# Decoder trunk on eight cores: squares of two chunks added in float32 before the ones product, in three of five norms

## The reference, cut to what matters

```python
def rmsnorm(x, g):
    xf = x.astype(jnp.float32)
    y = xf * lax.rsqrt(jnp.mean(xf * xf, axis=-1, keepdims=True) + EPS)
    return (y * g.astype(jnp.float32)).astype(x.dtype)
...
        h = rmsnorm(x, pre_mix_g[i])
        proj = h @ w_in[i] + b_in[i]
...
        x = x + rmsnorm(merged @ w_o[i], post_mix_g[i])
        h = rmsnorm(x, pre_ffn_g[i])
        f = jnp.square(jax.nn.relu(h @ w_ff1[i])) @ w_ff2[i]
        x = x + rmsnorm(f, post_ffn_g[i])
        gate = jax.nn.sigmoid(x @ w_ple_gate[i])
        e = p[i] @ w_ple_proj[i]
        x = x + rmsnorm(gate * e, post_ple_g[i])
```

## Time and profile before

| what | value |
|---|---|
| median of 3 runs | 2176.4 us (2175.73 to 2386.89) |
| the profiled execution's own time | 2177.32 us |
| its span on the slowest core (core 2) | 2175.4 us (2170.3 to 2175.4 over the cores) |
| TensorE busy | 2075.9 us (95% of the span) |
| VectorE busy | 1016.7 us (47%) |
| ScalarE busy | 848.1 us (39%) |

### The profile page before, as it was taken

One profiled execution on the slowest core, in us unless ns is written; L12 is line 12 of the kernel. 1 busy time (PEld: TensorE's weight loads), 2 busy tenths in 40 slices (PEclk: granted clock), 3 DMA queues, 4 the chain that ended last, 5 costly groups with the idle time before them and its releaser, 6 DMA issues.

```text
span 2175.4 us, 30026 instructions; the slowest of 8 cores (2170.3 to 2175.4 us)
## 1 busy us (share of the span) xinstructions
PE 2075.9 (95%) x10640; PEld 1043.8 (48%) x10818; DVE 1016.7 (47%) x1607; ACT 848.1 (39%) x1344; POOL 82.1 (4%) x156
## 2 busy tenths in 40 slices
PE   2999999999899999999989999999999999999996
PEld 1546666676544444444434444444444344444442
DVE  2438555302673856430374565541066385553027
ACT  2345154312645307321374522631166451543125
POOL 0000000000000000000000000000000000000000
PEclk8999999999999999999999999999999999999998
DMA  8234454434444363455576453554343344445342
GB/s 188 41 50 77 75 82 69 72 65 68 89 77 64 53 97 59 74 92 78 106 171 159 67 87 60 85 90 78 59 82 64 63 84 78 78 69 90 56 78 78
DMA packets 36325, 176.82 MB, mean 81 GB/s; under 512 B 3282, under 2 KB 6482, under 8 KB 18770
## 3 DMA queue, kind: packets, MB, share of 16 engines
q0 software_dynamic: 22912, 148.92, 42.6%
q1 hardware_dynamic: 13268, 25.98, 4.0%
HBM read 315.40 MB, written 8.39 MB: 149 GB/s over the span
## 4 chain that ended last, share of the span: by engine, by line
PE 92%; DMA 3%; ACT 2%; issue 2%; DVE 1%; SPq 0%; DVEq 0%; ACTq 0%; POOLq 0%
PE PS L676 80%; PE PS L794 5%; PE PS L593 3%; DMA XB<-xT 2%; PE PS L798 1%; PE PS L898 1%; PE PS L1108 1%; DMA WB<-wst 1%; PE PS L881 1%; ACT L1098 0%; PE PS L565 0%; ACT TMP L1098 0%; DVE U0A L906 0%; DVE XB L994 0%; ACT U1B L635 0%
## 5 line engine op out<-in xcount | busy, mean ns | idle before, releaser
L676 PE MATMUL PS<-U0A,WB 128*128 128x512 bf16 (+2 forms) x2907 | 525.5, 338 | 51.8 <-ACT U3A L833 22.6
L676 PE MATMUL PS<-U0B,WB 128*128 128x512 bf16 x2252 | 503.1, 379 | 3.1 <-ACT U56B L737 0.4
L676 PEld LDWEIGHTS PS<-U0A,WB 128*128 128x128 bf16 x2944 | 289.6, 99 | 271.4 <-issue 60.7
L676 PEld LDWEIGHTS PS<-U0B,WB 128*128 128x128 bf16 x2304 | 224.0, 98 | 264.2 <-issue 1.4
L1024 ACT ACTIVATE TMP<-PS 128x512 f32<-128x512 f32 (+1 forms) x256 | 151.3, 598 | 250.2 <-PE PS L676 245.4
L952 ACT ACTIVATE U1A<-PS 128x512 bf16<-128x512 f32 (+1 forms) x64 | 37.3, 603 | 391.6 <-PE PS L676 391.6
L487 POOL DMA_DIRECT2D WB<-wst x144 | 76.3, 530 | 2028.4 <-PE PS L676 1580.2
L676 PE MATMUL PS<-U2A,WB 128*128 128x512 bf16 (+1 forms) x631 | 120.5, 337 | 0.5
L676 PE MATMUL PS<-U3A,WB 128*128 128x512 bf16 (+1 forms) x637 | 118.0, 338 | 0.2
L676 PE MATMUL PS<-U2B,WB 128*128 128x512 bf16 x498 | 116.8, 379 | 0.9
L676 PE MATMUL PS<-U3B,WB 128*128 128x512 bf16 x504 | 117.1, 379 | 0.4
(11 more groups left out here) (184 smaller groups left out, 2242.1 us busy)
## 6 DMA issues: line engine op xcount, KB each, us to landing
WB<-wst POOLq DMA_DIRECT2D x136, 1024.0 KB, 10.8
XB<-xT SPq DMA_DIRECT2D x2, 2048.0 KB, 37.6
WB<-wst POOLq DMA_DIRECT2D x8, 512.0 KB, 6.3
outT<-XA SPq DMA_DIRECT2D x16, 256.0 KB, 2.9
outT<-XB SPq DMA_DIRECT2D x16, 256.0 KB, 6.9
XA<-xT SPq DMA_DIRECT2D x4, 528.0 KB, 9.4
U2A<-wsT SPq DMA_DIRECT2D x4, 512.0 KB, 6.2
BF<-bsbc SPq DMA_DIRECT2D x4, 512.0 KB, 7.0
```

The source lines that it names most:

```text
L676: return lambda e: e.matmul(PS[:, bk, 0:w], WB[:, b, k * kstride + fi * 128: k * kstride + (fi + 1) * 128], rhs(k, c0, c0 + w), start=(k = ...
```

## The change

Both sets of squares that are touched are now written by a method `square`. It writes the square of chunk dc in float32 into one of two scratch slots (dc even: the first, dc odd: the second), and after each odd chunk VectorE adds the two slots and writes the sum in bfloat16 as chunk dc // 2 of U1. The two slots are the upper half of U1 (chunks 4 to 7), seen as float32. `tail_ones` multiplies 4 chunks instead of 8 in post_mix, pre_ffn and post_ffn. Premix and post_ple keep their 8 products, and so does the sum over the halo. The eviction's other reader (L956 or L960) is unchanged.

```diff
-        def tail_ones(sq, rsq, cbl):
+        def tail_ones(sq, rsq, cbl, nc=8):
             bks = banks(len(cbl))
-            for dc in range(8):
+            for dc in range(nc):
                 fns = [lambda e, bk=bk, dc=dc, c0=c0, w=w: e.matmul(
-                    PS[:, bk, 0:w], ONEB[:], sq(dc, c0, c0 + w), start=(dc == 0), stop=(dc == 7))
+                    PS[:, bk, 0:w], ONEB[:], sq(dc, c0, c0 + w), start=(dc == 0), stop=(dc == nc - 1))
...
+            def square(self, dc, a, b, src, reads, psum, cbl, rp=()):
+                S = self.S
+                two = S.U[1].bitcast(F32).rearrange("p (c t) -> p c t", c=4)
+                t = [two[:, 2 + i, a - S.off[1]: b - S.off[1]] for i in range(2)]
+                rt = [S.rU[1][4 + 2 * i: 6 + 2 * i] for i in range(2)]
+                i = dc % 2
+                P.op("act", act_ns(b - a, psum), lambda e: e.activation(out=sv(t[i], cbl), in_=src, func=AF.Square),
+                     reads=reads, writes=rt[i] + list(rp))
+                if i:
+                    P.op("dve", dve_ns(b - a, False), lambda e: e.tensor_tensor(
+                        out=self.sq(dc // 2, a, b), in0=t[0], in1=t[1], op=ALU.add),
+                        reads=rt[0] + rt[1], writes=self.rsq(dc // 2))
...
@@ evac_O
-                P.op("act", act_ns(self.n, True), lambda e: e.activation(
-                    out=sv(self.sq(oc, a, b), self.cbs), in_=ps(bks, self.cbs), func=AF.Square),
-                    reads=rp, writes=self.rsq(oc) + rp)
+                self.square(oc, a, b, ps(bks, self.cbs), rp, True, self.cbs, rp)
...
@@ norm, post_mix, post_ple
-                bks = tail_ones(self.sq, self.rsq, self.cbs)
+                bks = tail_ones(self.sq, self.rsq, self.cbs, nc)
...
-                self.norm()
+                self.norm(4)
...
-                self.norm()
+                self.norm(8)
...
@@ ffn_eps
-                    P.op("act", act_ns(self.n, False), lambda e, dc=dc: e.activation(
-                        out=self.sq(dc, a, b), in_=S.x(dc, a, b), func=AF.Square), reads=[S.rX[dc]], writes=self.rsq(dc))
+                    self.square(dc, a, b, S.x(dc, a, b), [S.rX[dc]], False, blocks(a, a + 1))
...
@@ ffn_eps2, post_ffn
-                bks = tail_ones(self.sq, self.rsq, self.cbs)
+                bks = tail_ones(self.sq, self.rsq, self.cbs, 4)
```

More of the change, by code:

```diff
@@ L969, in o_half, with norm @@
                 w_done(S)
-            def norm(self):
+            def norm(self, nc):
                 S = self.S
                 a, b = self.r
-                bks = tail_ones(self.sq, self.rsq, self.cbs)
+                bks = tail_ones(self.sq, self.rsq, self.cbs, nc)
                 rsqrt_of(S.rb(a, b), S.rRB, bks, self.cbs)
```

## The result

| | before | after |
|---|---|---|
| profiled execution | 2177.32 us | 2157.07 us |
| median of the runs | 2176.4 us (first three) | 2157.9 us (2157.07 to 2158.86, 4 runs) |
| ratio to before, 95% interval | | 0.9917 (0.9893 to 0.9941) |
| TensorE, VectorE, ScalarE busy | 2075.9, 1016.7, 848.1 us | 2067.8, 1077.9, 848.2 us |

The kernel is 0.8% faster, which is less than the 2% that are held to tell two kernels apart by themselves, but the interval leaves out 1.

What follows compares the result with a forecast made beforehand. Behind the start-up, TensorE's list of matmuls was taken to bound the kernel. 2177.32 - 20.9 (matmuls) + 0.7 (ends of sums) + 0.6 (slots and plan) = 2157.7 us, median 0.9 us lower: 2157 us, range 2151 to 2173.

Steps and rivals of the forecast that it cites:

- Matmuls removed: In three norms of each of 8 passes, 84 wide and 24 narrow matmuls go from TensorE's list: 20.9 us.
- What bounds the kernel: Behind the start-up, TensorE's list of matmuls sets the length, with 2.6% idle; time taken off it shows in full.
- swallowed: Rival: something keeping its own time, such as a weight transfer, ends each stretch, so nothing gets shorter: 2176 us, chance 0.05.
- Squares and adds: ScalarE's squares into float32 cost 9 ns more at most; 96 VectorE adds of 0.69 us, 66 us, VectorE to about 1083.
- The wait at the end of a sum: Last add before the fourth product needs 1.05 us; cover 1.51, or 0.69 behind narrow matmuls: 0.7 us of waits together.
- The two scratch slots: Behind the outer half, third and fourth squares come up to 1.05 us later, hidden; 0.6 us allowed for planner errors.
- my second rival: Scratch pair blocks ScalarE in each round's B.o_half, adds queueing behind two residual operations: 41 us lost, 2198 us, chance 0.07.
- VectorE where it is full: B.o_half and 851.2 to 870.0 us of each round fill up; h has 3.3 and 4.8 us to absorb the backlog.
- the first rival: Adds come late behind 1.2 us residual operations in VectorE's full stretches, two sums a round: 10 us, 2167 us, chance 0.22.
- Sum: Whole kernel: 2177.32 - 20.9 + 0.7 + 0.6 = 2157.7 us, median 2157 us, 0.9% faster; this forecast's chance 0.66.
- What can be told from no change: All cases lie within 2% (2132.9 to 2219.9 us), about what a measurement can tell from no change: chance 0.97.
- TensorE busy about 21 us less: Sign expected in the profile after: TensorE's busy time falls about 21 us, with only tenths of new waits for VectorE.

Runs made afterwards that it cites:

- products alone: Changed kernel without its adds, squares written as before the change, those of chunks 4 to 7 left out of the four-product sums: 2154.99 us, ratio 0.9908 to before.
- Adds alone: Changed kernel with its adds kept but eight products per sum, each added chunk multiplied twice by a matrix of halves: 2177.6 us, ratio 1.0012 to before.

## Why the prediction was right or wrong

The time came out, and two things in the prediction did not: the cost of the new waits, 0.7 us at the ends of sums and 0.6 us for the slots and the plan, where 2.4 us were measured, because the cover was counted from the last square and not along the chain of four pairs through two slots; and the view that a gain of 0.9% is about what a measurement can't tell from none.

- *Matmuls removed, 20.9 us:* right. The counts are as forecast (112 in stream B; 108 fewer in all), and products alone gave 20.0 us.
- *What bounds the kernel:* right. Adds alone 1.0012, products alone 0.9908: time taken off TensorE's list showed in full. The gain was not swallowed.
- *Squares and adds:* right, 621 and 687 ns; VectorE 1077.9 us where 1083 were given. The rule that the prediction takes from the Trainium skill ("VectorE: DVE Perf Modes", What auto-detection actually checks) agrees with this case for the exact form: 687 ns with float32 inputs and a bfloat16 output, 421 ns all in bfloat16.
- *The wait at the end of a sum:* this step was wrong in post_mix. It took the cover to run from the last square, 1.51 us against a need of 1.05, as if the squares still came when their matmuls ended. With one pair of slots they come on a beat of 2.15 us from the outer half's burst: 4 pairs end 8.5 us after it (812.04 to 820.53), the fourth product stands at 820.41 + 0.65 = 821.06. The play in A.post_mix is 0.5 us, much as forecast, but by chance: it belongs to a chain of four adds, so a longer add counts four times (doubled adds: 4 x (2.94 - 2.15) = 3.2 us). In B.post_mix there was none, 0.17 us of waits in three rounds and 1.6 in the first (forecast 0 and 0.36); there ScalarE also writes A's h between the pairs. That 1.6 is over the microsecond that the prediction had named as the sign of being wrong, and with four slots it fell to 0.24. At post_ffn, where the squares lie 6.9 us apart, the step held: 0.24 us at the narrow one for 0.36.
- *The two scratch slots:* also wrong. I asked only for the banks ("hidden", and they were) and not for the sum at the end of the chain, though my second rival was about that very pair. Its place, B.post_mix, was right, its price, two residual operations before each add, wasn't met in the changed kernel. Doubled adds lengthen the chain, in A.post_mix too, and the kernel is 45 us slower, of which four slots take back 37.
- *VectorE where it is full:* right that it is full and that nothing broke. A window over the changed kernel's ff1 stretch:

```profile
845.50:862.70 17.20, 16.66 (x21) 1.00 0.20 41
```

  97% busy, and TensorE waits for nothing there. Late adds as a matter of load, the first rival, are not what the changed kernel pays for: even the doubled adds, once they have four slots, cost 8 us over the changed kernel and 11 over the one execution of single adds with four slots, not 45.
- *Sum:* 1.3 us of losses were given, 2.4 us of waits measured; start-up gave back 1.5. 2157 against 2157.9 us. The time is right in part because two misses of a microsecond cancelled: that is luck.
- *What can be told from no change:* wrong. The prediction gave 0.97 to "within 2%" as about what a measurement can't tell from none. The size was right, but the four runs of the changed kernel lie within 1.8 us and the ratio's interval, 0.9893 to 0.9941, leaves out 1: the kernel is faster, and a gain of 0.8% shows.
- *TensorE busy about 21 us less:* right of the list and wrong as a sign to look for: 8.1 us against the trace of before, in which records were missing, 21.6 us against the one of "Adds alone", which has them all.

## What to carry to other kernels

Where the chain is 92% matmuls, count the matmuls that go and multiply by the distance between neighbours; then look for cover at each place where the new producer ends. When a new step goes through a scratch buffer that is reused, count the buffer's beat over the whole sequence up to its consumer, not just the last link. Adding in the narrow type in place needed no scratch, cost 0.42 us and not 0.69, and let the sum go down to one product (about 2142 us, 1.5% under before; a fourth norm gave 1 us more). The price is that every partial sum is rounded to bfloat16, where the changed kernel rounds once for each pair.

## What I had not expected of the hardware

A wait of TensorE can cost more than its length: after the 3.7 us wait of the doubled adds at B.post_mix the granted clock was 0.50 from 858 to 864 us, though it was busy for 5.8 of those 6. In the changed kernel the longest new wait is 1.6 us, up to 315.39 us, and the clock stayed at 1.00 in every window from 310 to 330 us, as in those laid over the second round's sums.
